# Router's rows turned by halves inside the output projection, and plain product order after the first chunk

## What the reference computes

```python
    o = ...                                  # attention, [256, 1024]
    h = h + o @ w_out                        # the output projection
    xn = rms_norm_2(h, ln_ffn)               # x * rsqrt(mean(x*x) + eps) * gain
    g_prob = softmax(xn @ w_group + b_group)             # 4 groups, one is taken
    e_logits = (xn @ w_expert + b_expert)                # 32 experts, 8 in a group
    ...                                                  # two experts per token, weights comb
    hid = silu(xn @ w_gate[e]) * (xn @ w_up[e])
    h = h + sum over the chosen e of comb * (hid @ w_down[e])
    gate = sigmoid(rms_norm_2(h, ln_ple) @ ple_w_gate)
    h = h + gate * (p @ ple_w_proj)
```

## Time and profile before

| what | value |
|---|---|
| median of 3 runs | 1039.88 us (1039.24 to 1039.9) |
| the profiled execution, its own time | 1036.4 us |
| its span in the trace | 1034.6 us |
| PE, DVE, ACT busy in the span | 1009.3, 765.3, 699.1 us |
| granted clock of PE, mean | 1.0 |

### The profile page before, as it was taken

One profiled execution on the slowest core, in us unless ns is written; L12 is line 12 of the kernel. 1 busy time (PEld: TensorE's weight loads), 2 busy tenths in 40 slices (PEclk: granted clock), 3 DMA queues, 4 the chain that ended last, 5 costly groups with the idle time before them and its releaser, 6 DMA issues.

```text
span 1034.6 us, 17514 instructions
## 1 busy us (share of the span) xinstructions
PE 1009.3 (98%) x6141; PEld 843.8 (82%) x6141; DVE 765.3 (74%) x1350; ACT 699.1 (68%) x1207; POOL 110.2 (11%) x194
## 2 busy tenths in 40 slices
PE   7999999999999999999999999999999999999998
PEld 6887889999998877888688787877888688787877
DVE  5597666566666657877778888887887778888876
ACT  6675644444445536756698899857686598898955
POOL 9019000000000100300520000000000430000000
PEclk9999999999999999999999999999999999999999
DMA  9971047656554655004459999854514449999942
GB/s 294 298 258 64 1 155 231 183 182 195 178 174 163 190 182 205 2 17 148 182 213 326 337 338 335 303 183 145 164 58 163 183 161 322 331 345 334 330 141 72
DMA packets 107820, 209.25 MB, mean 202 GB/s; under 512 B 7864, under 2 KB 54432, under 8 KB 107488
## 3 DMA queue, kind: packets, MB, share of 16 engines
q1 hardware_dynamic: 105248, 204.04, 57.6%
q0 software_dynamic: 2064, 3.25, 1.2%
q10 hardware_dynamic: 432, 0.99, 0.3%
HBM read 207.19 MB, written 1.06 MB: 201 GB/s over the span
## 4 chain that ended last, share of the span: by engine, by line
PE 84%; DVE 7%; ACT 4%; DMA 2%; issue 2%; SPq 0%; ACTq 0%; DVEq 0%
PE bank L1774 18%; PE bank L919 12%; PE bank L1796 11%; PE bank L934 9%; PE bank L1420 9%; PE bank L1430 8%; PE bank L1068 4%; PE bank L1057 2%; PE bank L1032 2%; PE bank L812 2%; DVE weight_parts L969 1%; PE bank L1818 1%; PE bank L1598 1%; DMA expert_w<-in_moe_w_up 1%; PE bank L1637 1%
## 5 line engine op out<-in xcount | busy, mean ns | idle before, releaser
L1774 PE MATMUL bank<-expert_high,block_high 128*128 128x256 f32 x560 | 183.1, 328 | 1.5 <-ACT block_high L1717 1.3
L1701 DVE TENSOR_TENSOR expert_low<-expert_w,expert_high 128x1024 fp32r<-128x1024 f32 x140 | 164.9, 1221 | 8.0 <-ACT expert_high L1694 7.7
L1774 PE MATMUL bank<-expert_low,block_high 128*128 128x256 f32 x560 | 157.4, 282 | 0.0
L1694 ACT CAST expert_high<-expert_w 128x1024 fp32r<-128x1024 f32 x140 | 140.1, 1051 | 22.2 <-DMA expert_w<-in_moe_w_up 21.3
L1774 PE MATMUL bank<-expert_high,block_low 128*128 128x256 f32 x544 | 153.6, 282 | 0.0
L969 DVE TENSOR_TENSOR weight_parts<-ring,weight_parts 128x1024 fp32r<-128x1024 f32 (+3 forms) x116 | 122.3, 1081 | 40.2 <-ACT weight_parts L966 39.7
L966 ACT CAST weight_parts<-ring 128x1024 fp32r<-128x1024 f32 (+3 forms) x116 | 104.2, 928 | 63.8 <-PE bank L919 26.3
L919 PE MATMUL bank<-weight_parts,x_high 128*128 128x512 f32 (+3 forms) x544 | 145.7, 355 | 0.4 <-DVE weight_parts L969 0.4
L1796 PE MATMUL bank<-expert_w,junk 128*128 128x512 f32 x280 | 131.4, 593 | 0.0
L1774 PEld LDWEIGHTS bank<-expert_high,block_high 128*128 128x128 f32 x560 | 106.8, 191 | 18.5 <-issue 14.3
L1774 PEld LDWEIGHTS bank<-expert_low,block_high 128*128 128x128 f32 x560 | 106.8, 191 | 15.0 <-issue 15.0
(11 more groups left out here) (389 smaller groups left out, 1824.6 us busy)
## 6 DMA issues: line engine op xcount, KB each, us to landing
expert_w<-in_moe_w_gate SPq DMA_DIRECT2D x70, 512.0 KB, 5.7
expert_w<-in_moe_w_up SPq DMA_DIRECT2D x70, 512.0 KB, 7.3
expert_w<-in_moe_w_down SPq DMA_DIRECT2D x70, 512.0 KB, 5.6
ring<-in_w_ff SPq DMA_DIRECT2D x64, 512.0 KB, 3.9
ring<-in_w_in SPq DMA_DIRECT2D x16, 512.0 KB, 8.5
ring<-in_a_w_in SPq DMA_DIRECT2D x16, 512.0 KB, 6.5
ring<-in_ple_w_gate SPq DMA_DIRECT2D x12, 512.0 KB, 5.3
ring<-in_w_o SPq DMA_DIRECT2D x8, 512.0 KB, 5.4
```

Source lines behind the costliest of these rows:

```text
L1694: nc.scalar.copy(half_of(expert_high[:, b % 2, :], j), half_of(expert_w[:, b % DEPTH, 0:2048], j)).then_inc(ex_cast, 1)
L1701: nc.vector.tensor_tensor(half_of(expert_low[:, b % DEPTH, 0:2048], j), half_of(expert_w[:, b % DEPTH, 0:2048], j), half_of(expert_high[:, ...
L1774: mm = nc.tensor.matmul(to, x[:, b % 2, k, :], w[:, k], start=k == 0 and n == 0, stop=k == KB - 1 and n == 2)
```

## The change

The router's jobs `t_moe` become "whole": block k is columns 128k to 128k+127 of `h`, so the first two jobs need only the first 512 columns, which the first group of the output projection makes. PE turns the embedding and these two jobs inside the last group of the output projection, ahead of its chunk 1 (`inside_last`, `pe_turn_first_half`), after a wait for the add of the first group's second tile. ACT and DVE copy them ahead of the second group's adds and squares; only two jobs are left for after the projection. To match, the router's weights and a second copy of the gain (`route0`, `route1`) are loaded with row 128k+p on partition p, by SP just ahead of `sp_embed`, on the semaphore `embed_landed`, which now counts 64 per layer; the four loads at the start go. And in `pe_linear` only chunk 0 of a freshly turned group uses the order in parts; the other chunks wait for everything and use the plain order.

```diff
     def moe_and_ple(layer):
-        t_moe[layer] = turn(h, KB, [(turned_x, gains[f"ln_ffn{layer}"])])
+        t_moe[layer] = turn(h, KB, [(turned_x, gains[f"route{layer}"])], whole=True)
...
     for i in range(2):
-        load_small(route_w[:, i, :, 0:4], a["moe_w_group_2"][i].rearrange("(p k) n -> p k n", k=KB))
-        load_small(route_w[:, i, :, 4:36], a["moe_w_expert_2"][i].rearrange("(p k) n -> p k n", k=KB))
...
-    def pe_linear(pe, jobs, turned_by=(), ahead=None):
+    def pe_linear(pe, jobs, turned_by=(), ahead=None, inside_last=None):
         for group in zip(jobs[0::2], jobs[1::2]):
             for c, number in enumerate(group[0]["splits"]):
+                if inside_last is not None and group[1] is jobs[-1] and c == 1:
+                    inside_last()
...
-                if made_of is not None and "dve" in made_of["counts"] and "act" in made_of["counts"]:
+                if c == 0 and made_of is not None and "dve" in made_of["counts"] and "act" in made_of["counts"]:
                     pe_chunk_in_parts(pe, group, c, number, made_of)
...
     def pe_route(pe, layer):
+        pe.wait_ge(embed_landed, 64 * (layer + 1))
...
+    def pe_turn_first_half(pe, layer):
+        pe_turn(pe, t_embed[layer])
+        pe.wait_ge(*took_at((l_nsa_o if layer == 0 else l_moba_o)[1]))
+        pe_turn(pe, t_moe[layer][:2])
+
     def pe_moe_and_ple(pe, layer):
-        pe_turn(pe, t_embed[layer])
-        pe_turn_tiles(pe, t_moe[layer], [took_at(j) for j in (l_nsa_o if layer == 0 else l_moba_o)[-2:]])
+        pe_turn_tiles(pe, t_moe[layer][2:], [took_at(j) for j in (l_nsa_o if layer == 0 else l_moba_o)[-2:]])
...
     def act_moe_and_ple(act, layer):
         act_square_tile(act, n_moe[layer], 0, took_at(added[0]))
-        take_turn(act, t_embed[layer], "act")
         act_square_tile(act, n_moe[layer], 1, took_at(added[1]))
-        take_turn(act, t_moe[layer], "act")
+        take_turn(act, t_moe[layer][2:], "act")
...
     def dve_moe_and_ple(dve, layer):
-        take_turn(dve, t_embed[layer], "dve")
-        take_turn(dve, t_moe[layer], "dve")
+        take_turn(dve, t_moe[layer][2:], "dve")
...
+    def sp_route(sp, layer):
+        for dest, src in ((gains[f"route{layer}"][:, :], a["ln_ffn_2"][layer].rearrange("(k p) -> p k", k=KB)),
+                          (route_w[:, layer, :, 0:4], a["moe_w_group_2"][layer].rearrange("(k p) n -> p k n", k=KB)),
+                          (route_w[:, layer, :, 4:36], a["moe_w_expert_2"][layer].rearrange("(k p) n -> p k n", k=KB))):
+            sp.dma_start(dest, src, allow_slow_non_contiguous=True).then_inc(embed_landed, 16)
...
+        sp_route(sp, 0)
         sp_embed(sp, 0)
...
-        pe_linear(pe, l_nsa_o, t_mix2, ahead={1: turn_last(t_mix2, c_taken, 4)})
+        pe_linear(pe, l_nsa_o, t_mix2, ahead={1: turn_last(t_mix2, c_taken, 4)},
+                  inside_last=lambda: pe_turn_first_half(pe, 0))
...
         nc.scalar.preload_act_table(ACT.Sqrt)
+        take_turn(act, t_embed[0], "act")
+        act.wait_ge(embed_landed, 64 * 0 + 64)
+        take_turn(act, t_moe[0][:2], "act")
         act_moe_and_ple(act, 0)
...
         dve_split_expert(dve, 0, 1)
+        take_turn(dve, t_embed[0], "dve")
+        dve.wait_ge(embed_landed, 64 * 0 + 64)
+        take_turn(dve, t_moe[0][:2], "dve")
         take_linear(dve, l_nsa_o[2:], "dve")
```

More of the change, by code:

```diff
@@ L229, in build_program @@
     for name in ("norm_mix_g", "norm_ffn_g", "ln_mix0", "ln_ffn0", "ln_ple0", "kv_norm", "ln_mix1", "ln_ffn1",
-                 "ln_ple1"):
+                 "ln_ple1", "route0", "route1"):
         gains[name] = sb(f"gain_{name}", [P, KB])
@@ L1594, in pe_embed @@
             wait_turned(pe, t_embed[layer])
-            pe.wait_ge(embed_landed, 16 * (layer + 1))
+            pe.wait_ge(embed_landed, 64 * (layer + 1))
             wait_turned(pe, t_moe[layer])
@@ L2140, in _ @@
             sp_chunk(sp, n)
+        sp_route(sp, 1)
         sp_embed(sp, 1)
@@ L2407, in _ @@
         pe.wait_ge(biased, n_heads[0])
-        pe_linear(pe, l_moba_o, t_mix3, ahead={1: turn_last(t_mix3, mixed, n_heads[0] // 4)})
+        pe_linear(pe, l_moba_o, t_mix3, ahead={1: turn_last(t_mix3, mixed, n_heads[0] // 4)},
+                  inside_last=lambda: pe_turn_first_half(pe, 1))
         pe_moe_and_ple(pe, 1)
@@ L2593, in _ @@
         nc.scalar.preload_act_table(ACT.Sqrt)
+        take_turn(act, t_embed[1], "act")
+        act.wait_ge(embed_landed, 64 * 1 + 64)
+        take_turn(act, t_moe[1][:2], "act")
         act_moe_and_ple(act, 1)
@@ L2826, in _ @@
         dve_split_expert(dve, 1, 1)
+        take_turn(dve, t_embed[1], "dve")
+        dve.wait_ge(embed_landed, 64 * 1 + 64)
+        take_turn(dve, t_moe[1][:2], "dve")
         take_linear(dve, l_moba_o[2:], "dve")
```

## The result

The changed kernel takes 1046.12 us, the median of 8 runs (1043.39 to 1050.26), beside 1039.71 for the kernel before in the runs next to them (8 runs). The ratio is 1.0072, 95% interval 1.0053 to 1.0091: slower by 0.7%, or 6.4 us between the medians, 7.5 by the ratio, where 2.5 were forecast. The sign was right, the size was not, and 1046.1 lies above the range.

The account below looks back on a forecast made before the run. PE's queue was taken to bound the kernel, except in two post-projection tails set by the second group's add and ACT's work after it; 2 x 0.82 + 0.83 = 2.5 us on the median 1039.88 gave 1042.4, range 1039.2 to 1044.0.

Parts of the forecast that it names:

- The turns inside the projection: Output projection's last group: embedding turns, wait and eight router turns delay PE by 0.47 + 0.67 + 0.79 = 1.93 us per layer.
- The wait behind L993: Inside each output projection's last group: PE idles 0.6 to 0.7 us for the first group's second add; sign of being right.
- What ACT and DVE save behind it: Tail behind the output projection: fewer ACT copies, so root and everything up to the experts come only 0.82 us later per layer.
- Plain order: Chunk 1 of `l_c` and both gates starts later, by 0.35, 0.36 and 0.12 us; 0.83 in all, free elsewhere.
- The loads: SP's queue during attention: three router loads fit into its 32 us hole; cost 0, bound 0 to 10 us.
- The sum: Whole kernel: 2 x 0.82 + 0.83 = 2.5 us slower, bounds 2.2 to 3.3; forecast's chance 0.58.
- Half the loss: Rival, output projection: wait met otherwise, each layer loses 0.15 us, in all 1.1, giving 1041.0; chance 0.24.
- long turns: Rival, inside the projection: turns cost their full flight, 2.1 us more per layer, giving 1046.6; chance 0.06.
- late loads: Rival, behind the attention: router loads still running at 782 delay everything, at 10 us giving 1052; chance 0.05.
- cheaper products: Rival, plain-order chunks: shorter second load of a stationary block; at 0.0135 us saved per product, 1037.7; chance 0.07.
- a tail that hangs on something other than ACT's squares and copies: Behind the output projection: named sign of being wrong, as the tail was taken to hang on ACT's squares and copies.

Follow-up runs that it names:

- the filler: Changed kernel plus eight products of zeros in PE's gap ahead of the logits' turn, replacing nothing; 1043.23 us, 1.0047 of the kernel before.
- the kernel with the rows' order alone: Kernel before, with DVE copying the logits' rows ahead of its root steps instead of behind them; 1037.66 us, 0.9998.
- the memset early: Changed kernel, with GpSimd clearing the experts' sums after the output projection's first group's add instead of after its end; 1041.08 us, 1.0031.

## Why the prediction came out too small

**The turns inside the projection**, 1.93: right. PE's next product would have begun at 482.98 and begins at 484.92, 1.94 later; the second group's adds come 2.13 later (493.42 against 490.24 + 1.05), inside the bounds of 1.87 to 2.21; a slower first chunk behind the turns (2.85 for 2.72) is most of the difference. The wait behind L993 is there, 0.46 in the row because the embedding's turns are counted in full (0.63).

**What ACT and DVE save behind it**, 0.82: this is the step that failed: the root starts 0.82 later, "and with it DVE's root, the logits' copy and everything up to the experts". Its first half holds within the bounds of 0.76 to 1.10: the root comes 1.08 and 1.04 later, since the square of tile 1 came 1.80 later in place of 1.59 and the two copies took 0.82 in ACT's timeline, so 0.73 was saved of 1.55 (0.78 forecast). Its second half does not: the root's steps were taken over from before at their old length, although the change moved them under a memset that starts at the same add. The logits' copy is 2.13 later, not 0.82, and 1.05 of it is L762. GpSimd's memset has no place in the forecast; an engine off the critical path with 3.5 us of work at just that date was reason enough to ask.

**The clock** had no term at all. The forecast took every duration behind the tail from before. The drop in layer 0's tail is worth 1.7; the filler puts the share of the drops at 2.6 us of the 7.5, roughly.

**Plain order**, 0.83: the place and the later start were right (0.39 for 0.35), the size was not: 1.3. Left out was the restart behind the gap, and the last gate, 0.26 to 0.30 for 0.12.

**The loads**, 0: right. SP issued the three loads of layer 0 from 403.92 to 413.37 (the group's weights alone took 5.51 us of its queue) and had nothing to issue until 464.00.

**The sum.** Without the memset's hold and without the drops the change costs 3.4 us by the ledger and 3.2 by the ratio, where 2.5 were forecast, with bounds of 2.2 to 3.3. The rest is the two waits: 2.1 us of hold (1.05 a layer) and 2.6 of clock. 3.2 + 2.1 + 2.6 = 7.9, beside 7.5 measured with an interval of 5.5 to 9.5. The 2.6 is the least certain of the three.

**The rivals.** Half the loss, long turns, late loads and cheaper products didn't come: the wait is there, the eight turns lie within 0.84, PE waits for no load, and the products keep 0.227 once they run (36 in 8.17 before; 487.93 to 493.39 for the last 24 after). What the forecast named as a sign of its own failure, a tail that hangs on something other than ACT's squares and copies, is what happened.

## What to carry to other kernels

When a change makes a chain shorter at one place, read what every other engine does at the new dates, the idle-looking ones too: here a step that cost 0.2 us, because it came as another engine's long instruction ended, cost that instruction's rest when it came earlier. Look at how long the matmul engine waits after a change, not only at who waits for it; a wait of 2.3 us cost another 1.7 in the products behind it in three tails of four, and moving work into a gap only moves the gap if the work is taken from a place where it covered another. When the turns by halves come with a loss of 0.7% in one arrangement and with none in another, the idea isn't what was measured; the dates around it were.

## What the runs showed of the hardware

- A GpSimd memset of 128x4096 (3.51 us) held DVE's `tensor_scalar` on 128x2 elements in SBUF to its end, for 1.05 and for 2.97 us, and held neither `reciprocal` nor `tensor_tensor`, nor a `tensor_scalar` that reads PSUM (DVE's two router copies at 494.71 take 0.88 us with the memset beside them, and 0.88 with the memset early).
- The kernel before has drops of its own: over a third of its runs show a mean clock of 0.996 to 0.998. In the trace of the kernel with the rows' order alone, which had one, it lies at 415 to 425 us, not in the tails, behind a stretch in which PE was busy for 4.66 and 4.09 of 5 us (windows as above). There it cost some 3.1 us: from 417.20 to 427.92 between two marks that lie 7.61 apart in the kernel before. What sets it off isn't known: in the changed kernel's trace PE is busy for the same 4.09 us at 410 to 415, and no drop follows.

```profile
405.00:410.00 5.00, 4.66 (x39) 4.28 (x39) 4.28 (x17) 2.95 (x4) 0.00 (x0) 1.00 1.03 383
410.00:415.00 5.00, 4.09 (x38) 3.74 (x37) 4.45 (x13) 3.53 (x7) 0.00 (x0) 1.00 0.79 295
415.00:420.00 5.00, 5.00 (x36) 4.67 (x37) 3.61 (x15) 3.01 (x14) 2.15 (x3) 0.76 0.01 3
420.00:425.00 5.00, 5.00 (x28) 3.37 (x27) 2.39 (x13) 2.09 (x9) 1.09 (x2) 0.56 0.00 0
```

- So a difference of 0.2% between two versions can be the clock alone, and the mean granted clock of each run has to be read beside its time.
